# Two transformer blocks in fp32 on one core: feed-forward pairs with the second matrix first, passes of 4, 3 and 4 pairs, and inner activations at a multiple of 64 bytes

## The reference

```python
# first block, for each of its two layers (mod = silu(c) @ ada_w[l] + ada_b[l])
x = x + g1 * (mix @ w_out[l])
h = rmsnorm(x, norm_ffn_g[l]) * (1.0 + sc2) + sh2
f = (jax.nn.silu(h @ ffn_w1[l]) * (h @ ffn_w3[l])) @ ffn_w2[l]
x = x + g2 * f
# second block, for each of its two layers
x = layer_norm(ALPHA * x + mix, ln1_g[i], ln1_b[i])
gate, up = jnp.split(x @ w_ffn_in[i], 2, axis=-1)
ffn = (jax.nn.silu(gate) * up) @ w_ffn_out[i]
ple = (p[i] @ w_ple[i]) * jax.nn.sigmoid(x @ w_ple_gate[i])
x = layer_norm(ALPHA * x + ffn + ple, ln2_g[i], ln2_b[i])
```

## Time and profile before

| | |
|---|---|
| median of 3 runs | 2623.67 us (2622.88 to 2628.45) |
| the profiled execution's own time | 2625.39 us |
| its span in the profile | 2623.6 us |
| mean granted TensorE clock | 0.969 of full speed |
| busy: PE, DVE, ACT, POOL | 2464.9, 1656.4, 1064.8, 1084.3 us |
| FFN of the layers: 1, 2 (first block) | 289.0 to 673.1, 898.8 to 1274.4 us |
| FFN of the layers: 3, 4 (second block) | 1577.9 to 1931.4, 2243.4 to 2596.9 us |

### The profile page before, as it was taken

The page is one execution under the profiler, slowest core; times in us unless marked ns, Lnnn a source line. Parts: engine busy times, 40 slices in busy tenths (PEclk is TensorE's granted clock), DMA queues, the critical chain, the costliest instruction groups (busy, mean ns, idle before and its releaser), DMA issues.

```text
span 2623.6 us, 33681 instructions
## 1 busy us (share of the span) xinstructions
PE 2464.9 (94%) x13254; PEld 2044.7 (78%) x13254; DVE 1656.4 (63%) x2422; ACT 1064.8 (41%) x1729; POOL 1084.3 (41%) x621
## 2 busy tenths in 40 slices
PE   7799699999999889999999989999989998999997
PEld 4576588988676778888787768888869776888885
DVE  5798883865577884644487476454467747655445
ACT  4225443433425533333443554333334354443432
POOL 0333444354234345354244345535413534554541
PEclk8899899999999989999999999999989999999998
DMA  7513233564322233233332113323322211232321
GB/s 274 177 58 119 81 126 125 178 199 129 114 81 81 96 129 113 81 113 97 83 80 73 57 57 97 113 81 113 97 78 72 69 59 59 90 113 81 120 93 45
DMA packets 243350, 268.78 MB, mean 102 GB/s; under 512 B 19592, under 2 KB 211832, under 8 KB 242936
## 3 DMA queue, kind: packets, MB, share of 16 engines
q1 hardware_dynamic: 243192, 266.63, 31.7%
HBM read 264.51 MB, written 2.10 MB: 102 GB/s over the span
## 4 chain that ended last, share of the span: by engine, by line
PE 81%; DVE 11%; ACT 3%; POOL 2%; issue 2%; DMA 1%; SPq 0%; DVEq 0%; ACTq 0%; POOLq 0%
PE bank L2675 25%; PE bank L2677 24%; PE bank L2676 24%; DVE m_cv L2105 2%; PE bank L3262 1%; POOL w_lo L1531 1%; POOL u_t_lo L1682 1%; DVE g_acc L1785 1%; PE bank L3180 1%; PE bank L3295 1%; DVE u_t_raw L2629 1%; PE bank L2974 1%; DVE small L1910 0%; POOL k_lo L1542 0%; DVE u_full L1836 0%
## 5 line engine op out<-in xcount | busy, mean ns | idle before, releaser
L1542 POOL TENSOR_TENSOR k_lo<-raw,k_hi 128x512 fp32r<-128x512 f32 x288 | 417.3, 1457 | 523.4 <-ACT k_hi L1001 522.6
L1001 ACT ACTIVATE k_hi<-raw 128x512 fp32r<-128x512 f32 x528 | 326.4, 628 | 593.6 <-PE bank L2677 448.8
L2675 PE MATMUL bank<-h_hi,k_lo 128*128 128x512 f32 (+1 forms) x1232 | 428.2, 348 | 36.4 <-DVE u_act L1982 25.4
L1531 POOL TENSOR_TENSOR w_lo<-raw,w_hi 128x2048 fp32r<-128x2048 f32 x53 | 252.3, 4760 | 499.1 <-ACT w_hi L947 472.0
L2676 PE MATMUL bank<-h_lo,k_hi 128*128 128x512 f32 (+1 forms) x1232 | 426.5, 346 | 0.0
L2677 PE MATMUL bank<-h_hi,k_hi 128*128 128x512 f32 (+1 forms) x1232 | 425.8, 346 | 0.0
L2675 PE MATMUL bank<-h_hi,w_lo 128*128 128x512 f32 (+1 forms) x784 | 322.7, 412 | 45.4 <-DVE h_lo L1891 13.6
L2676 PE MATMUL bank<-h_lo,w_hi 128*128 128x512 f32 (+1 forms) x784 | 312.5, 399 | 0.0
L2677 PE MATMUL bank<-h_hi,w_hi 128*128 128x512 f32 (+1 forms) x784 | 312.3, 398 | 0.0
L2675 PEld LDWEIGHTS bank<-h_hi,k_lo 128*128 128x128 f32 x1232 | 235.5, 191 | 67.3 <-DVE u_act L1982 25.8
L1931 DVE TENSOR_TENSOR k_lo<-raw,k_hi 128x512 fp32r<-128x512 f32 x240 | 249.1, 1052 | 59.4 <-ACT k_hi L1001 59.2
(11 more groups left out here) (391 smaller groups left out, 4722.6 us busy)
## 6 DMA issues: line engine op xcount, KB each, us to landing
raw<-in_ffn_w SPq DMA_DIRECT2D x60, 1024.0 KB, 5.3
raw<-in_w_ffn_in SPq DMA_DIRECT2D x44, 1024.0 KB, 5.1
raw<-in_w_in SPq DMA_DIRECT2D x34, 1024.0 KB
b_raw<-in_ada_w SPq DMA_DIRECT2D x32, 1024.0 KB, 5.2
raw<-in_w_ffn_out SPq DMA_DIRECT2D x16, 1024.0 KB, 5.1
z_a<-in_ada_w SPq DMA_DIRECT2D x4, 2048.0 KB, 14.1
g_raw<-in_ada_w SPq DMA_DIRECT2D x8, 1024.0 KB, 5.2
raw<-in_w_out SPq DMA_DIRECT2D x8, 1024.0 KB
```

What stands on the lines that cost most here:

```text
L1001: act.activation(hi, src, ACT.Copy).then_inc(s.f_hi.up, 1)
L1531: pool.tensor_tensor(b.w_lo[p][:, 0:n], b.raw[p][:, 0:n], b.w_hi[p][:, 0:n].bitcast(F32), ALU.subtract)\
L1542: pool.tensor_tensor(lo, src, hi.bitcast(F32), ALU.subtract).then_inc(s.f_lo.up, 1)
L2675: pe.matmul(out, wlo, xhi, start=start, stop=False)
```

## The change

1. The units of a pair change places: plain, then seven. Plain loads raw buffer 0 and seven raw buffer 1. `gated`, the second silu and f_hi, f_lo of a pair now follow its seven, at parts 0 and 1 of the next unit. In the early plan units 0 and 1 are mixed as before, with the roles exchanged.
2. The passes are 4, 3 and 4 pairs, with one pair ahead at the second alone: p0 s0 ... p3 s3, 4 downs, p4 s4 ... p7 s7, 4 downs, p8 s8 ... p10 s10, 4 downs.
3. Plain uses banks 2 and 3 for even pairs, 6 and 7 for odd ones. The folds move to bank 4, columns 256 and on.
4. `LAST_SLOTS` is now the two halves of the ring in turn: the last pass's first unit has slots 0 to 3, its second 4 to 7, and the highs and lows of the second are made once the last seven has run. As before, the three units after the first go bank by bank for all their pairs.
5. In the gate stage of the second block POOL makes t_lo in two pairs, each after one w_lo, and ACT makes t_hi in the gate loop. The matmuls of `pe_shift_sums` come before the last six of the last unit.
6. `pick4` goes into the tile `eps`, so all that is placed behind it moves down by 32 bytes: f_hi to 128640, f_lo to 149120, both multiples of 64. `u.at += 32` leaves t_hi and t_lo where they were. e_hi and e_lo (second block) go from multiples of 64 to 32 over one.

The number of matmuls and their sizes are the same.

```diff
-PASSES = [range(0, 4), range(4, 8), range(8, PAIRS)]
+PASSES = [range(0, 4), range(4, 7), range(7, PAIRS)]
+AHEAD = [0, 1, 0]
 SPARE = 5
 RING = 8
 M1, M6, M7, M5, M4, M2, M3 = range(7)
-LAST_SLOTS = [(1, 2, 3), (4, 5, 6), (0, 1, 2), (7, 4, 5)]
+LAST_SLOTS = [(0, 1, 2, 3), (4, 5, 6, 7)] * 2
...
-            upto = min(pairs[-1] + 2, PAIRS)
+            upto = pairs[-1] + 1 + AHEAD[n]
             for i in range(done, upto):
-                self.units += [("seven", i, 0), ("plain", i, 0)]
+                self.units += [("plain", i, 0), ("seven", i, 0)]
...
-            self.seq[:11] = ([(0, M1), (0, M2), (0, M3)] + [(1, n) for n in range(4)]
-                             + [(0, M6), (0, M7), (0, M5), (0, M4)])
+            self.seq[:11] = ([(1, M1), (1, M2), (1, M3)] + [(0, n) for n in range(4)]
+                             + [(1, M6), (1, M7), (1, M5), (1, M4)])
...
+    def banks(self, u):
+        kind, i, _ = self.units[u]
+        if kind == "seven":
+            return 0, 1, 4, 5
+        first = (6 if i % 2 else 2) if kind == "plain" else 2 * (u % 2)
+        return first, first + 1
...
-        b.eps = place("eps", [P, 4], F32)
+        b.eps = place("eps", [P, 8], F32)
         b.wff = place("wff", [P, 4 * KD + 28], F32)
-        b.pick4 = place("pick4", [P, 4], F32)
+        b.pick4 = b.eps[:, 4:8]
...
         b.u_row, b.u_third = u("row", [P, T]), u("third", [P, T // 2])
+        u.at += 32
...
-        early = plan.early and u < 2
         if kind == "seven" and part == M6:
             first(u, i)
-        if kind == "seven" and part == M3 and not early:
+        if kind == "seven" and part == M2 and not (plan.early and i == 0):
             silu(i, 1)
-        if kind == "plain" and part == 0 and not early:
-            silu(i, 0)
-        if early and (u, part) == (0, M4):
-            silu(i, 1)
-            silu(i, 0)
-        if part == 0 and u and plan.units[u - 1][0] == "plain":
-            hidden(plan.units[u - 1][1])
+        if u and plan.units[u - 1][0] == "seven":
+            old = plan.units[u - 1][1]
+            if part == 0:
+                if plan.early and old == 0:
+                    silu(old, 1)
+                silu(old, 0)
+            if part == 1:
+                hidden(old)
...
-    for t in range(4):
-        act.wait_ge(*s.t2_d(l, t + 1))
-        act.activation(b.t_hi[:, t, :, :], b.t_raw[:, t, :, :], ACT.Copy).then_inc(s.t2_h.up, 1)
...
             split(16 + k // 2)
+            for t in (k - 1, k):
+                act.wait_ge(*s.t2_d(l, t + 1))
+                act.activation(b.t_hi[:, t, :, :], b.t_raw[:, t, :, :], ACT.Copy).then_inc(s.t2_h.up, 1)
...
-        if part == 0 and u and plan.units[u - 1][0] == "plain":
+        if part == 1 and u and plan.units[u - 1][0] == "seven":
             hidden(plan.units[u - 1][1])
...
     for t in range(4):
+        if t % 2 == 0:
+            split(16 + t // 2)
...
-    for j in range(16, 18):
-        split(j)
...
-    def gated(u, i):
-        dve.wait_ge(*s.stepped(n, plan, u, 3))
+    def gated(i):
         if i:
             dve.wait_ge(*s.fl(n, 2 * i))
         for m in range(2):
             dve.wait_ge(*s.f_silu(n, 2 * i + (1 if m else 2)))
-            dve.tensor_tensor(b.f_full[:, m, :], b.f_act[:, m, :], bank[2 + m][:, :], ALU.mult)\
+            dve.tensor_tensor(b.f_full[:, m, :], b.f_act[:, m, :], bank[(6 if i % 2 else 2) + m][:, :], ALU.mult)\
                .then_inc(s.f_gated.up, 1)
     for t, (u, part) in enumerate(plan.seq):
         kind, i, j = plan.units[u]
         last = t == plan.end(u)
...
+        if part == 0 and u and plan.units[u - 1][0] == "seven":
+            gated(plan.units[u - 1][1])
...
-        if part == (M7 if plan.early and u == 0 else M5) and u + 2 < plan.tail and plan.units[u + 2][0] == "seven":
+        if part == (M5 if kind == "seven" else 0) and u + 2 < plan.tail and plan.units[u + 2][0] == "seven":
             dve_sums(dve, e, lay, u + 2)
-        if kind == "plain" and last and not (plan.early and u == 1):
-            gated(u, i)
-        if plan.early and (u, part) == (0, M4):
-            gated(1, 0)
...
-            dve_sums(dve, e, lay, 0)
+            dve_sums(dve, e, lay, 1)
...
-        if u == 8:
+        if u == 7:
...
-        return three(pe, bank[2 * (u % 2) + m][:, :], b.k_hi[:, at, v], b.k_lo[:, at, v], x[0][:, tile, :],
+        return three(pe, bank[plan.banks(u)[m]][:, :], b.k_hi[:, at, v], b.k_lo[:, at, v], x[0][:, tile, :],
...
-        if u < 2:
+        before = [v for v in range(u) if set(plan.banks(v)) & set(plan.banks(u))]
+        if not before:
             return
-        kind, i, j = plan.units[u - 2]
+        kind, i, j = plan.units[before[-1]]
         if kind == "seven":
-            pe.wait_ge(*s.f_part(n, 5 * i + 5))
+            pe.wait_ge(*s.f_part(n, 5 * i + (4 if plan.units[u][0] == "down" else 5)))
         elif kind == "plain":
             pe.wait_ge(*s.f_gated(n, 2 * i + 2))
         else:
...
-        outermost = u >= plan.tail + 1
+        first = len(pairs) - (4 if u > plan.tail else 1)
...
-            if outermost or k == len(pairs) - 1:
+            if k >= first:
...
-        ks = range(len(pairs)) if outermost else (len(pairs) - 1,)
         for m in range(2):
-            for k in ks:
+            for k in range(first, len(pairs)):
+                if m and k == len(pairs) - 1 and halfway is not None:
+                    halfway(u, 1)
...
-    def fold(row, acc, cols, ready):
+    def fold(u, acc, cols, ready):
+        row, off = bank[FOLD_AT[0]], FOLD_AT[1]
+        last = max(i for kind, i, _ in lay.plan.units[:u + 1] if kind == "seven")
+        pe.wait_ge(*s.f_part(lay.ffn, 5 * last + 2))
         pe.wait_ge(*ready)
...
-    def halfway(u):
-        if u == lay.plan.tail + 2:
+    def halfway(u, at):
+        if (u, at) == (lay.plan.tail + 2, 0):
             pe.wait_ge(*s.n2_sum(l, 3))
             pe.matmul(bank[6][:, :], b.ones[:, :], b.r[:, :], start=True, stop=True).then_inc(s.n2_mean.up, 1)
-    def between(u):
-        if u == lay.plan.tail + 3:
+        if (u, at) == (lay.plan.tail + 3, 1):
             pe_shift_sums(pe, e, l)
-    pe_ffn(pe, e, lay, None, between, halfway)
+    pe_ffn(pe, e, lay, None, None, halfway)
```

47 lines of the change are left out of this document (26 added, 21 removed).

## The result

The changed kernel takes 2612.45 us (median of 6 runs, 2610.49 to 2616.8), the kernel before, run beside it, 2627.34 (6 runs, 2622.88 to 2629.32). The ratio is 0.9945, with 95% interval 0.9935 to 0.9955: 14.9 us less. The direction is the forecast one and the time lies inside the range, though only by half a microsecond, but the gain is 14.9 where 33 was forecast: the prediction's sum is wrong.

A forecast was written before the change was run, and what follows sets the result against it. TensorE, busy 94% of 2623.6 us, was taken as the bound, so only shorter matmuls or PE waits pay. The terms summed to -33.0 us, giving 2591 us for the median, with a range of 2572 to 2613.

The forecast's parts named there:

- A: FFN matmuls with f moving: on multiples of 64 bytes they take h's pace, 6.6 ns less each; -13.3 us.
- B: Start of FFN 1 and 2: PE's stall for u_act goes, -30.4, with 8.2 given back by DVE; net -22.2 us.
- C: Gate stage of layers 3 and 4: w_lo ahead of t_lo cuts PE's wait to 1.9 us; -8.2 in all.
- D: New bank hand-offs of p4 and p8 behind down units: 1.1 us lost at 8 places, +8.8.
- E: First down unit of the last pass: PE waits 2.2 us for POOL's last f_lo, four times; +8.8.
- F: Ends of the FFNs: longer last pass and earlier shift sums hide DVE's long sum beside POOL's w_lo; -6.9 us.
- G: Layer 2's wait for mod, sums before the FFN from raw buffer 1, folds in bank 4: costed at 0.
- I give back 4.1 per FFN: In B, FFN 1 and 2: DVE's weigh piece (5.6 us) and a low part exceed its free time, costing 4.1 each.
- Rival 2: DVE, 90% busy, keeps the start of FFN 1 and 2: half of 22.2 given back, 2602 us; chance 0.18.
- Rival 3: Slower by the clock: hand-offs and late f_lo grow to 6.0 us each at 12 places, 2650 us; chance 0.06.
- Both signs that the prediction named as its own failure: FFN windows of layers 3 and 4 not shorter, or those of 1 and 2 shorter by less than 10 us each.

The follow-up runs named there:

- thin: Changed kernel with DVE's weigh pieces in the first block's FFNs made on 8 of their 512 columns; 2597.95 us.
- defer: Changed kernel with DVE's four low parts of unit 2 at the start of FFN 1 and 2 moved behind u_third; 2605.84 us.
- f_first: Changed kernel with f_hi and f_lo of a pass's last pair made at part 0 of the down unit, ahead of other parts; 2597.19 us.
- banks: Changed kernel with the banks of plain exchanged from pair 4 on, so no plain follows a down unit in the same banks; 2592.9 us.
- before_moved: Kernel before with the addresses alone: f_hi and f_lo put on multiples of 64, t left where it was; 2615.94 us.
- f_back: Changed kernel with all tiles of the FFN at 32 bytes over a multiple of 64 again, t as it was; 2617.39 us.
- t_aligned: Changed kernel with t_hi, t_lo and what is placed behind them 32 bytes lower, on multiples of 64; 2617.64 us.
- again: The changed kernel once more, unchanged, for a second profile; 2612.91 us.

## Why the prediction was wrong

By its own steps; the last column is worked out from the stage table, the waits and their half clock, in the two profiled executions. For a wait the loss is counted, some 0.2 us more than PE's idle time.

| term | forecast | measured |
|---|---|---|
| A, addresses | -13.3 | -13.4 in the FFNs |
| B, start of FFN 1 and 2, net | -22.2 | about -12 |
| C, gate stages | -8.2 | about -11 |
| D, hand-offs | +8.8 | +11.3 |
| E, last f_lo | +8.8 | +9.2 |
| half clock behind E in FFN 3 and 4 | 0 | +3.4 |
| F, ends of FFNs, with 0.9 of half clock | -6.9 | about -2 |
| G, mixing stages ahead of FFN 1 and 2 | 0 | +5.8 |
| sum | -33.0 | -9 (spans: -9.6) |

**The step that failed most is B's "I give back 4.1 per FFN".** The stall went as said (no wait for u_act), and with it 30.4 us. But some 18 came back, not 8.2. FFN 1 changed by +1.2: take out the addresses (-3.4), D (+5.4) and E (+2.3), and -3.1 is left of a stall that cost 16.85, so 13.8 came back there. In FFN 2 it is -7.9 + 3.4 - 2.1 - 2.3 = -8.9 of 13.6, so 4.7, near the forecast. I had costed DVE's lateness at one place, the parts, by a share of free time, 2.2 us in a pair. What the runs showed is that PE waits for DVE, or for POOL held up beside it, at several places one after another: in FFN 1 for u_t_lo, POOL's k_lo, two folds and a small one for u_row, 9.2 us in all where it was 2.3 outside the stall, and once more at the hand-off counted in D. The half clock on a working PE adds 6.1 to that: 8.8 us now, 2.7 before without the part behind the stall. thin takes 11.5 off FFN 1, defer 6.9. Rival 2, "DVE keeps the start", with half of B given back, had the place, the engine and the size (11 us more than B, here 10 more); its time, 2602, is 10 too low, since other terms failed besides.

The stall itself went with some luck. B took the load and the sums to come when they did. Counted from the start of the FFN, the load came 1.5 us later (323.95 - 291.68 against 319.81 - 289.02), and the parts were ready 1.3 later than forecast, more than the slack of 0.1. Nobody waited because PE came 3.0 us later as well, held up by u_t_lo and k_lo. B's starting point was also too simple: FFN 1 and FFN 3 are not "the same matmuls" (2060 and 1981 records of matmuls, those of the folds among them), so not all of the 52.6 us was there to gain.

**E: number and path right, the clock behind it left out.** I counted four low parts and one more, then f_lo, "some 10.4 with waits between"; it is 10.45, and PE's wait is 2.24 for a forecast 2.2. f_first, which takes the one more and the wait before it away, takes 2.0 of that off. What failed is that I put the clock behind it at nothing, although rows 8 and 9 showed half clock behind a wait of 4.3; here it stands behind waits of 2.2. Rival 3 had this mechanism, at the wrong size: 3.4 us of loss in FFN 3 and 4, not 59.

**D** was right at seven places (0.9 to 1.0 lost at each) and wrong at one (4.3 idle), where DVE had something else to do first. Its worth is greater than its waits: banks takes some 17 us out of FFNs and gate stages.

**F: the collision did not go, it moved along.** I took the 3.9 as hidden by the longer pass. But POOL's w_lo, ACT's u_act and DVE's sum come forward together, so DVE's sum takes 4.63 us again and PE waits 2.96 for it instead of 3.79, now in the middle of the last unit, with half clock behind it from 1930.0 on. No run took this wait away.

**C** was too small: the wait is 1.20, not the 1.9 forecast, and 0.95 us between gate stage and FFN are gone as well (1569.52 to 1569.74, where it was 1576.67 to 1577.85). Why PE paused there before is not shown. Undoing the order costs 4.7 per stage but 6 in all, so some of it is given back in the FFNs.

**A** was right in mechanism and size where it was measured. It fell short as a step of the sum: alone it is worth 10.3, since the mixing stages are some 3 us longer per profile, and in the new order its undoing costs 4.9. **G**, costed at nothing, is where the former went; as these waits change from profile to profile, its 5.8 is that of this pair of profiles and may be less in the medians. G's "folds in bank 4" failed too: their waits for u_third, 3.0 us in FFN 1 and 2, are new, and stand in B above.

Both signs that the prediction named as its own failure came true: FFN 1 and 2 did not get shorter by 10 us each (+1.2 and -7.9), and the windows of layers 3 and 4 did not get shorter at all (+8.6 and +4.4; they now hold the matmuls of the shift sums, but D, E and the clock behind E take some 6 us in each, more than the 3.5 of A).

## What to carry to other kernels

When a change removes a large stall, list what each engine had been doing during it, and follow that work to every later place where PE waits for that engine, not to the next one only: the stall was its cover. A short wait of PE is worth more than its length once half clock stands behind it, and two mends that take away the same half clock don't add up. Before blaming a late result on its input, compare when the input was ready with when the engine that uses it came free: here a wait of ACT for a load stood next to the late f_lo, but POOL's own queue set its time.

## What the runs showed of the hardware

- The pace of matmuls depended on the address of the moving operand, with a sign that depended on the columns: 512 columns took 226.7 ns on a multiple of 64 bytes and 233.3 at 32 over one (before against before_moved, after against f_back); 256 columns took 120 on a multiple and 117.5 at 32 over (after against t_aligned). No other offsets were run.
- Half clock stood behind waits of 2.2 us of PE in the FFNs in some profiles (after: behind f_lo) and not behind nearly the same waits in others (banks, FFN 3 and 4; f_back, FFN 4). In FFN 3 and 4 it differed between kernels, not between the two profiles of the changed kernel. At the start of FFN 1 a wait of 3.0 us for k_lo had half clock with it in again and none in banks, f_back and f_first, behind a wait of 0.9 to 1.1 in all four.
- DVE and POOL working side by side have two outcomes in one kernel: a POOL instruction of 1.47 us takes 5.44 beside an unbroken run of DVE's, or DVE's ten of 6.71 take 14.48 beside a row of POOL's.
